# A hybrid decoder step: the 80-column projection on raw turned rows, and the fifth block's values gathered earlier

## What is computed

```
n = x * rsqrt(mean(x*x) + 1e-6) * norm_mix          # RMSNorm, per row of x
p = n @ w_in                                        # 4688 columns, split into
                                                    # a_u, a_v, b_q, b_k, b_v, i_q, i_k (64), i_w (16)
score = sum_h i_w[h] * relu(i_q[h] . i_k)           # indexer: picks the top keys of each query
b_out = softmax(q k_sel + bias) v_sel               # sparse attention over the picked keys
h = x + concat(a_out, b_out) @ w_out
h = h + cross_attention(rms_norm(h), memory)
h = h + experts(rms_norm(h))                        # top-1 of 4 groups, top-2 of 4 experts
```

## Time and profile before

| | us |
|---|---|
| runs | 1297.85, 1298.12, 1294.4 |
| median | 1297.85 |
| profiled execution | 1298.46 |
| its span in the profile | 1296.3 |
| PE busy | 1230.6 (95%) |
| DVE busy | 490.5 (38%) |
| mean granted TensorE clock | 0.974 |

### The profile page before, as it was taken

One profiled execution on the slowest core, in us unless ns is written; L12 is line 12 of the kernel. 1 busy time (PEld: TensorE's weight loads), 2 busy tenths in 40 slices (PEclk: granted clock), 3 DMA queues, 4 the chain that ended last, 5 costly groups with the idle time before them and its releaser, 6 DMA issues.

```text
span 1296.3 us, 13643 instructions
## 1 busy us (share of the span) xinstructions
PE 1230.6 (95%) x5650; PEld 585.9 (45%) x5650; DVE 490.5 (38%) x959; ACT 189.6 (15%) x397; POOL 51.0 (4%) x67
## 2 busy tenths in 40 slices
PE   7999999999999988999997999999999999999996
PEld 4344443344444455677775664333333333333332
DVE  5000175089564553011124561243333333333335
ACT  2012233300221343000023330000000000000000
POOL 0002000000000012100000000000000000000000
PEclk8999999899999989999998998899999999999999
DMA  7835422345332349754456358999999999999961
GB/s 246 322 130 138 138 98 90 140 162 189 104 130 98 102 161 359 267 137 140 147 177 250 135 204 309 412 427 427 427 427 425 426 428 428 427 427 425 428 266 74
DMA packets 71130, 332.01 MB, mean 256 GB/s; under 512 B 13564, under 2 KB 17436, under 8 KB 54492
## 3 DMA queue, kind: packets, MB, share of 16 engines
q1 hardware_dynamic: 54624, 282.65, 55.5%
q0 software_dynamic: 8464, 41.42, 8.3%
q10 hardware_dynamic: 7980, 7.05, 2.2%
HBM read 320.61 MB, written 10.49 MB: 255 GB/s over the span
## 4 chain that ended last, share of the span: by engine, by line
PE 80%; DVE 8%; DMA 8%; ACT 3%; issue 1%; POOL 0%; DVEq 0%; ACTq 0%
PE PS L650 20%; PE PS L1217 16%; PE PS L943 14%; PE PS L1274 8%; PE PS L1181 5%; PE PS L627 3%; DMA NC<-in_w_up 2%; DMA ring<-in_w_up 2%; DVE X L1827 2%; DVE top L1826 2%; PE PS L768 1%; PE PS L891 1%; PE PS L1263 1%; PE PS L1185 1%; DMA X<-in_cache_v,ids 1%
## 5 line engine op out<-in xcount | busy, mean ns | idle before, releaser
L650 PE MATMUL PS<-ring,NC 128*128 128x512 f32 x704 | 325.5, 608 | 1.6 <-issue 1.6
L650 PEld LDWEIGHTS PS<-ring,NC 128*128 128x128 f32 x704 | 130.4, 193 | 156.2 <-issue 155.1
L943 PE MATMUL PS<-NC,ring 128*128 128x288 f32 x768 | 190.5, 407 | 1.6 <-issue 0.5
L1217 PE MATMUL PS<-ring,NC 128*64 128x512 f32 x768 | 178.2, 602 | 4.0 <-DMA ring<-in_w_up 2.5
L943 PEld LDWEIGHTS PS<-NC,ring 128*128 128x128 f32 x768 | 144.3, 190 | 42.0 <-issue 2.9
L2149 DVE TENSOR_TENSOR X<-X,PS 128x1024 f32<-128x1024 f32 x64 | 78.1, 1221 | 148.6 <-PE PS L1181 148.6
L1217 PEld LDWEIGHTS PS<-ring,NC 128*64 128x64 f32 x768 | 51.4, 137 | 123.3 <-issue 121.7
L1274 PE MATMUL PS<-ring,NC 128*64 128x512 f32 x384 | 87.8, 611 | 0.5 <-ACT NC L1713 0.5
L1711 ACT ACTIVATE NC<-PS,small 64x512 f32<-64x512 f32 x16 | 10.9, 681 | 437.2 <-PE PS L1217 437.2
L1181 PE MATMUL PS<-XNN,NC 64*128 64x512 f32 x256 | 72.3, 641 | 0.3 <-DVE XNN L2191 0.3
L1217 PE MATMUL PS<-XNN,NC 128*64 128x512 f32 x128 | 59.0, 599 | 1.5 <-DMA NC<-in_w_up 1.5
(11 more groups left out here) (407 smaller groups left out, 1086.4 us busy)
## 6 DMA issues: line engine op xcount, KB each, us to landing
ring<-in_w_gate SPq DMA_DIRECT2D x24, 2048.0 KB, 18.6
ring<-in_w_up SPq DMA_DIRECT2D x24, 2048.0 KB, 22.0
ring<-in_w_down SPq DMA_DIRECT2D x24, 2048.0 KB, 20.8
ring<-in_w_in SPq DMA_DIRECT2D x36, 1024.0 KB, 4.9
ring<-in_w_out SPq DMA_DIRECT2D x16, 1024.0 KB, 5.1
XNN<-in_w_gate SPq DMA_DIRECT2D x8, 2048.0 KB, 19.4
NC<-in_w_up SPq DMA_DIRECT2D x8, 2048.0 KB, 22.5
XNN<-in_w_down SPq DMA_DIRECT2D x4, 2048.0 KB, 21.6
```

The costliest lines, as they stand in the source:

```text
L650: last = mm(acc(n, t)[:, 0:width], lhs[:, kt, t * 128:(t + 1) * 128], slot(m)[:, k, 0:width], start=kt == 0, stop=kt == KT - 1)
L943: last = mm(PS[:, j, 0:NT], slot(m)[:, k, 128 * j:128 * j + 128], src[:, kt, :], start=kt == 0, stop=kt == width * 4 - 1)
L1217: last = mm(PS[64 * half:64 * half + 64, 2, :], XT[:, 4 * (kt // 4 % 2) + kt % 4, kt // 8, :], w, start=kt == 0, stop=kt == KT - 1)
```

## The change

Item 0 no longer goes through the weight ring. Its weights come by one load into W80, an area of XN; DVE multiplies them by the gains (norm_mix per slice of 128 rows), and PE multiplies them with the raw turned rows xT. After the eighth slice PE spreads the inverse roots (`row_scales`); ACT takes the unscaled result out of PSUM, DVE multiplies it by the roots, and ACT makes kiT from that in SBUF. The gain transpose stands between the first and the second tile of x. The ring's count starts at 4, so item 1's four loads have no slot to wait for. Item 1 is now the one that waits for the normalised slices.

In the attention stage the gather of values 4 stands ahead of the gather of keys 4 in POOL's queue, with its wait; POOL waits for all of values 4 to 7 before it issues the first half of xts; and PE waits for DVE's half of the turned keys only before the second range of keys.

```diff
+        W80 = XN[:, 0:80 * KT].rearrange("p (k n) -> p k n", k=KT)
@@ sync
+                if n == 0:
+                    sp.dma_start(W80, wv).then_inc(S("w80_in"), 16)
+                    n = 4
+                    continue
-                    if n >= NSLOT:
+                    if n >= 2 * NSLOT:
                         sp.wait_ge(S("ring_free"), n - NSLOT + 1)
@@ gpsimd
+                if b == 4:
+                    pool.wait_ge(S("misc_free"), groups_through(("item", N_OUT - 1)))
+                    gather(values(4), cv, 4, "v_in1")
                 if b >= 4:
                     pool.wait_ge(S("kt_ready"), 4 * (b - 3))
-            pool.wait_ge(S("misc_free"), groups_through(("item", N_OUT - 1)))
-            gather(values(4), cv, 4, "v_in1")
             pool.wait_ge(S("s_qk"), 2)
...
             pool.wait_ge(S("s_logits"), 2)
+            pool.wait_ge(S("v_in1"), 64)
@@ tensor
+                        if g == 7:
+                            pe.wait_ge(S("rs_diag"), 1)
...
-                pe.wait_ge(S("x_laid_a"), 4)
-                pe.wait_ge(S("gain_in"), 64)
-                tr(PS[:, 7, 0:64], gain_rows, ident[0:64, 0:64]).then_inc(S("gain_t"), 1)
-                pe.wait_ge(S("rs_diag"), 1)
+                    if t == 0:
+                        pe.wait_ge(S("gain_in"), 64)
+                        tr(PS[:, 7, 0:64], gain_rows, ident[0:64, 0:64]).then_inc(S("gain_t"), 1)
+                pe.wait_ge(S("x_laid_a"), 8)
+                pe.wait_ge(S("x_laid_v"), 5)
+            def row_scales():
+                pe.wait_ge(S("rs_diag"), 2)
                 for t in range(3):
                     last = mm(PS[:, 6, t * 128:t * 128 + ROWS[t]], ones_row[0:ROWS[t], :],
...
                         if n == 0:
-                            pe.wait_ge(S("n_laid"), kt + 1)
-                            last = mm(acc(0, 0)[0:width, 0:NT], slot(m)[:, k, 0:width], nT[:, kt, :],
+                            if kt == 8:
+                                row_scales()
+                            last = mm(acc(0, 0)[0:width, 0:NT], W80[:, kt, :], xT[:, kt, :],
                                       start=kt == 0, stop=kt == KT - 1)
                             continue
+                        if n == 1:
+                            pe.wait_ge(S("n_laid"), kt + 1)
...
-                pe.wait_ge(S("kt_laid"), 8 * (x + 1))
                 for i, (a, z) in enumerate(KEYCUT):
+                    if i == 1:
+                        pe.wait_ge(S("kt_laid"), 8 * (x + 1))
@@ scalar
                 if n == 0:
-                    A(spart[0:width, 0:NT], PS[0:width, ps, 0:NT], ACT.Copy).then_inc(S("part"), 1)
-                    A(kiT[0:64, :], PS[0:64, ps, 0:NT], ACT.Copy)
-                    A(kiT[64:128, :], PS[0:64, ps, 0:NT], ACT.Copy).then_inc(S("acc_out"), 1)
+                    A(spart[0:width, 0:NT], PS[0:width, ps, 0:NT], ACT.Copy).then_inc(S("rowsq"), 1)
+                    act.wait_ge(S("part"), 1)
+                    A(kiT[0:64, :], spart[0:64, 0:NT], ACT.Copy)
+                    A(kiT[64:128, :], spart[0:64, 0:NT], ACT.Copy).then_inc(S("acc_out"), 1)
@@ vector
+                dve.wait_ge(S("gain_t"), 1)
+                V.tensor_copy(gcol[:, 0:48], PS[:, 7, 0:48]).then_inc(S("rs_diag"), 1)
                 dve.wait_ge(S("x_in2"), 16)
...
+                dve.wait_ge(S("w80_in"), 16)
+                dve.wait_ge(S("rs_diag"), 1)
+                TT(W80, W80, bc(gcol[:, 0:16], 2, [128, KT, 80]), ALU.mult).then_inc(S("x_laid_v"), 1)
                 dve.wait_ge(S("rowsq"), 2)
                 rsqrt(xrs, rx, xss, 1.0 / D, rt)
...
-                dve.wait_ge(S("gain_t"), 1)
-                own(V.tensor_copy(gcol[:, 0:48], PS[:, 7, 0:48]))
...
                 for k in range(KT):
                     STT(nT[:, k, :], xT[:, k, :], gcol[:, k:k + 1], PS[:, 6, 0:NT], ALU.mult, ALU.mult).then_inc(S("n_laid"), 1)
+                dve.wait_ge(S("rowsq"), 3)
+                TT(spart[0:80, 0:NT], spart[0:80, 0:NT], PS[0:80, 6, 0:NT], ALU.mult).then_inc(S("part"), 1)
```

More of the change, by code:

```diff
@@ L640, in products @@
                     m = ring_n[0]
-                    pe.wait_ge(S(f"ring_in{m % NSLOT}"), 16 * (m // NSLOT + 1))
+                    if n:
+                        pe.wait_ge(S(f"ring_in{m % NSLOT}"), 16 * (m // NSLOT))
                     for k in range(4):
@@ L1382, in evacuate @@
                 width = ITEMS[n][2].shape[2]
+                if n == 1:
+                    act.wait_ge(S("acc_out"), 1)
                 if n and n in FOLDED:
```

## The result

| | before | changed |
|---|---|---|
| median, us | 1298.12 (9 runs) | 1289.82 (9 runs) |
| profiled execution, us | 1298.46 | 1288.2 |
| its span | 1296.3 | 1286.4 |
| PE busy | 1230.6 (95%) | 1225.5 (95%) |
| DVE busy | 490.5 (38%) | 492.5 (38%) |

The ratio is 0.9931, with a 95% interval of 0.9916 to 0.9946, that is 9.0 us less (7.0 to 10.9); the medians are 8.3 apart. Forecast: 9.0.

A forecast was written before the change was run, and what follows sets the result against it. TensorE (PE) bounds the kernel, 80% of the chain. Head 2.8 plus tail 6.2 give 9.0 us: profiled 1298.46 becomes 1289.5, less 0.6 for the median 1288.9; range from 1285.8 up to rivals A and B (1291.5, 1293.8).

The forecast's parts named there:

- Head: Item 0's projection from raw turned rows and W80 ends earlier: 2.8 us, between 1.5 and 3.0.
- the cap: At item 0's fold: ACT issues small DMAs until 31.67 before its copy, so the head gives at most 3.0 us.
- signs listed for being wrong: Projection starting after 16, fold waiting, second value product waiting over 2 us or at 1.2 GHz, longer experts' stage.
- Tail: Sample attention: earlier score products and value landings, second value product at full clock; 6.2 us, bounds 3.4 and 7.2.
- (a): Attention: score products start right behind the transposes, without waiting for DVE's half; 0.8 us and 0.5 us.
- (b): Attention: block 4's values, gathered ahead of its keys, move in the idle DMA stretch and hold up nobody.
- (c): Attention: 1.75 MB leave the values' stream (4.3 us), which starts 0.8 earlier; second value product gains 4.8 us.
- (d): Attention: PE has no gap over 1.5 us, so the second value product takes 4.2, not 5.6: 1.4 us.
- A: Rival: head's clock returns late or fold waits longer, half the tail's clock gain missing: 6.3 us, 1291.5; chance 0.14.
- B: Rival in attention: a gather's time is its own latency, block 7's again takes 11.46: 4.1 us, 1293.8; chance 0.12.
- C: Rival: nothing arrives, because something downstream is tied to a time that doesn't move: 1297.9; chance 0.08.
- D: Rival at the head: W80 lands last, at 25.9, behind other loads; slower, 1301.7; chance 0.04.

The follow-up runs named there:

- values5_early: Changed kernel with block 5's values gathered right behind block 4's, ahead of the second keys; ratio 0.994 against the kernel before.
- act_loads_late: Changed kernel with 17 of ACT's small loads moved behind its copy of item 0; ratio 0.993 against the kernel before.
- after_again: The changed kernel run once more without any edit; ratio 0.9942 against the kernel before, 7.5 us less.
- head_only: Kernel before with only the change's projection, its attention left as it was; ratio 0.9977 against the kernel before.
- saved_late: Kernel before with one edit: POOL issues the half of the saved rows after values 4 to 7 have landed; ratio 0.9993.
- saved_undone: Changed kernel without the wait that holds the saved rows until the last values have landed; ratio 0.9943 against the kernel before.
- keys_early: Kernel before with one edit: PE waits for DVE's half of the turned keys only before the second range of keys; ratio 0.9984.
- tail_only: Kernel before with only the change's sample attention edits, its projection left as it was; ratio 0.9961 against the kernel before.

## Why the prediction was right, and where it was off

**Head, 2.8 forecast, 2.97 in the traces, 3.0 in the ratio.** Right, and for the reason given last. W80's scaling: forecast 13.1 to 14.65, measured 13.26 to 14.75. The start, 14.9, measured 14.89. The clock was the step that failed: PE stood 1.73 us (forecast 1.1) and the clock stayed up, so the projection ended at 23.79 and not at 25.0. In values5_early it did fall, after 1.77 us; there the projection started at 14.58 and item 1 began at 25.00, as forecast. With the clock up the cap decided (fold at 32.68, forecast 32.65); with the clock down the fold stood right behind item 1's first quarter, without a wait, at 32.96 (forecast 32.8). So this error cost some tenths. That the cap is ACT's issuing was shown by act_loads_late. The prediction let it stand still; in fact ACT came to its copy between 31.40 (values5_early) and 32.83 (after_again, where its loads began 1.05 us later than in the changed kernel and the fold waited until 33.77). The 2.97 is an average over such executions. Of the signs listed for being wrong, two showed: the fold waited (1.03), because the projection was done ahead of the cap, and the stage behind the attention was longer in this pair of traces, which is the clock's doing (below). Constants: issued at 13.20, they landed 7.0 us later, at 20.2 (forecast 21.0), and item 1 waited for none of them. The normalised slices, 19.90 to 26.79, held nobody.

**Tail, 6.2 forecast, 5.0 in the traces, 5.1 in the ratio.** (a) In head_only, where this edit is undone, each set of score products waits for DVE (0.88 us, twice); in the changed kernel for ACT (0.25, twice). That is 1.26 of 1.3 forecast, more evenly split than 0.8 and 0.5:

```profile
479.89 0.62 PE L915 MATMUL PS<-X,ring 128*32 128x512 f32 x2 [0.88 <-DVE ring L1958]
```

```profile
475.67 0.62 PE L918 MATMUL PS<-X,ring 128*32 128x512 f32 x2 [0.25 <-ACT ring L1632]
```

(b) Values 4 go out 0.21 us behind the first turned key and neither keys 4 nor PE wait for it. (c) is the step that was mis-sized: 4.3 us for 1.75 MB, and 0.8 for the earlier start. In the four traces with values 4 late block 7's values land 42.5 to 42.9 us behind the first turned key (before 42.74), in seven with values 4 ahead 39.3 to 40.4 (40.4 in the changed kernel's own, 39.3 in after_again). On average that is 3.0 us earlier, where 5.1 was forecast. The 1.05 MB of values 4 at 402 GB/s make 2.6 of it. The saved rows' part, 1.7, doesn't exist: saved_late and saved_undone agree on that in their traces. Of the 0.8 for the earlier start about 0.4 is left, and keys_early, which has that edit alone, shows none of it (42.89 for 42.74); how much it gives stays open. The reading error was to take "the engines are full until the values land" as "the values land when these bytes are through". The last gather thins out first: in the eleven traces that record its landing, all but seven of its packets have ended 0.7 to 1.9 us before it, and the last packet 0.3 to 0.5 us before, and other bytes fill that time. Why a few packets come so late stays open. The windows of after_again show it too, with the landing at 511.97:

```profile
510.00:511.00 1.00, 0.28 (x1) 0.09 (x1) 0.00 (x0) 1.00 (x4) 0.00 (x0) 1.00 0.39 164
511.00:512.00 1.00, 0.00 (x0) 0.00 (x0) 0.00 (x0) 0.04 (x1) 0.00 (x0) 1.00 0.04 16
```

The first value product was forecast 0.9 us earlier. It came 0.88 earlier in tail_only and after_again (32.07 and 32.06 behind the first turned key, formerly 32.94), about 0.6 in saved_undone, act_loads_late and values5_early, and only 0.02 in the changed kernel's own trace, where block 3's values held it until 499.00. (d) Right for the second product, 4.27 in every kernel with values 4 early; missed for the first, which the clock struck in five of seven executions (5.5 to 7.2 us). Nor was it true that PE has no gap over 1.5 us: it waited 2.48 before the first product of the changed kernel and 1.63 before the second of after_again. On the other hand the second product of before, 5.59, was a mild case: head_only and saved_late show 7.17 and 7.18. The first makes the gain smaller than forecast and the second makes it larger; that the two errors have opposite signs is luck.

**What passes on.** Forecast 1:1. head_only and tail_only multiply to the whole within the intervals, so no loss is seen. In the pair of traces alone the rest was 3.9 longer, but the clock took 4.3 more there; with the clock's part taken off the rest is 757.5 and 757.1.

**The rivals.** A (head 1.5): the clock can fall there, but the cap hides it. B, a gather's time is its own latency: wrong. In keys_early block 7's gather goes out 1.3 us earlier behind the first turned key (29.99, formerly 31.28) and takes 12.90 in place of 11.46, and with values 4 gone ahead it takes 9.70 to 10.6; the bytes of the gathers in front of it set its end. Where the four traces with values 4 late issue it at 29.99 to 31.28, it lands at 42.5 to 42.9. C: the gain arrived. D, W80 landing behind the ring's loads: in the changed kernel the engines are full at 12.5 to 13 (365 GB/s), and W80, issued at 2.14, landed 11.0 us later, at 13.1, not at 25.9; the last of its four loads had landed at 12.6 in the kernel before. By then 4 MB were queued behind it, but not from the start: SP issued 1 MB at 2.74 and the other three from 10.32 to 11.62. The Trainium skill (DMA: Bandwidth & Descriptors, Two DMAs through the same engine are not ordered), by which the descriptors of one queue start in order on a DMA engine, spoke against D, and the trace agrees.

The two measured stages sum to 8.0, forecast 9.0. The head gave 0.2 more than forecast. In the tail, on average over the same traces as the 5.0, the second value product started 2.6 us earlier (40.2 behind the first turned key, formerly 42.8) where 4.8 was forecast, for the two reasons under (c) and the first product's clock; and it was 2.4 us shorter where 1.4 was forecast, because the 5.59 of before's own trace is a mild case. The ratios, 0.9931 and 0.9942, hold both 8.0 and 9.0, so the time alone wouldn't have found the missing 1.7. That the first ratio gives 9.0 to the tenth is luck; the second gives 7.5.

## What to carry to other kernels

Where an engine is freed earlier, look for the next reader of its result and for what that reader does meanwhile: here a queue of small DMA issues on ACT, readable in the trace before, held the head's gain near 3.0 whatever the clock did. Full DMA engines up to a landing don't prove that the bytes queued behind delay it; check how long after its issue the transfer lands when nothing follows, and when its last packets end. Subtract two profiles stage by stage, take each stage's lost clock off before comparing, and trust a stage that the change doesn't touch only as a measure of the scatter.

## What the runs showed of the hardware

- A wait of PE alone doesn't tell whether the clock falls. At the head, after the same work, it stayed up over 1.73 us (changed) and fell over 1.77 us (values5_early). In the attention it stayed up over waits of 1.17, 1.40, 1.63 and 1.66 us and fell over 1.30 (saved_undone), 1.82 (keys_early) and 2.48. Shortly ahead of each wait before a first value product stood another one, of 0.25 to 0.94 us. With matmuls of no use in the wait it stayed up in three of three.
- Between the head and the attention, 433.4 to 441.9 us for nearly the same instructions: single quarters of items take 7.06 us or 8.8 to 10.0. The slow ones lie at the same few places in all traces; whether each comes changes from one execution of a kernel to the next. Less the lost clock, the stage takes 428.0 to 430.5 us.
- Block 7's values (an indirect gather of 1.05 MB) landed 11.46 to 12.90 us after their issue when all eight gathers of values came in one stream, and 9.70 to 10.6 with values 4 gone ahead, with or without 1.18 MB of saved rows queued behind them. All but seven of its packets (8 KB each) have ended 0.7 to 1.9 us before it counts as landed, the last one 0.3 to 0.5 us before (eleven traces).
- A direct load of 640 KB (2.14) with 1 MB queued right behind it in the same queue and 3 MB more from 10.32 on landed at 13.1, while the engines ran at 365 GB/s. In four loads with no more work behind them, the same bytes had landed by 12.6.
- Issuing a load of 0.1 or 0.5 KB kept ACT's queue for about 0.7 us (17 such small loads from 19.91 to 31.69 in the changed kernel).
